# First mixer of a two-block transformer kernel: block-diagonal keys, one score product per unit

## Chip, cores and metric

One core of a Trainium2 chip runs the whole kernel. The time is the device time of one execution in microseconds; the lower it is the better. Three executions of the kernel before took 1032.47, 1033.88 and 1033.93 us, median 1033.88.

## What is computed

Two transformer blocks follow one another on 256 tokens of width 1024, all in float32. The change lies in the first block's mixer. Its one half is a differential attention of 4 heads. Each head has two sets of queries and keys of 64 dimensions, a rotary on the first 16 of them, and one set of values of 128:

```python
def block(qblk):                       # 128 queries at a time
    s = jnp.einsum('bqhmd,bkhmd->bhmqk', qblk, k)
    a = jax.nn.softmax(s, axis=-1)
    w = a[:, :, 0] - lam * a[:, :, 1]
    return jnp.einsum('bhqk,bkhe->bqhe', w, v)
```

There is no mask: every query sees all 256 keys. The mixer's other half is a gated linear recurrence (HGRN2, both directions), computed here in nine levels of blocks. Both halves are normalised per head, joined and multiplied by an output matrix. Then comes a gated feed-forward layer, a per-layer embedding gate and the second block.

## The kernel before

**Engines and queues.** The order of work is written out by hand, one program for each engine, with semaphores between them. Large matrices come through a ring of three slots (`raw`, 256 columns of a weight, 1 MB). ScalarE casts a slot to its high part (`hi`, line 497), VectorE subtracts to get the low part (`lo`, line 961), and TensorE multiplies high and low parts in fp32r with the high and low parts of the activations, three products for each tile. The next transfer into a slot starts when its low part is made. GpSimd casts one slot at the start (line 483) and is idle after that.

**Before the scores.** The input projection has 16 slots. The columns of `dq` and `dk` (slots 8 to 11) go transposed into `qT` and `kT`: 128 partitions hold the two 64-dimension sets of a head, with 4 heads and 256 tokens along the free dimension. TensorE puts one level of the recurrence behind each of the slots 6 to 13 (`level`, line 1915: eight float32 products of 128x128 by 128 columns) and the last two levels, 7 and 8, between the products of slot 14. VectorE prepares a level (`diffs`, `scaled`), and places the products into `AT` under a mask (`place`, line 1126). Log keys of the recurrence lie in `nb` under the name `kin`; the differences of level 7 (semaphore `lev_diff` at 8) read them last.

**Rotary.** `rotate(n)` on VectorE turns a pair of heads of `qT` (n = 0, 2) or `kT` (n = 1, 3) in place: a shuffle into `rot1`, two multiplications and an add (lines 1152 to 1155), all of 128 partitions by 512 elements. Rotations 0 and 1 stand in front of the placing of level 6, which TensorE's level 8 waits for; 2 and 3 stand behind the placings of levels 7 and 8, each in front of the maximum of unit 0 or 1.

**Units.** A unit n is a head (n // 2) and a block of 128 queries (n % 2); there are 8. Its two softmaxes share one PSUM bank, 256 columns each; two banks alternate. `scores(n, m)` (line 1927) multiplies the 64 partitions of set m. The second set's product waits for the first one's semaphore. VectorE takes the maxima of both sets in one reduction (`da_max`, line 1215); ScalarE takes two exponentials with sums (`da_exp`, line 668); VectorE makes two diagonal matrices of 1/sum and -lambda/sum (`da_diag`, lines 1219 to 1223); TensorE transposes and combines both sets by four float32 products with them (`da_pt`, line 1994); ScalarE copies the result (`da_copy`, line 677); TensorE multiplies by the values once both units of a head are there (`da_pv`, line 2002). A unit's score waits for the exponentials two units before.

**TensorE's order around it** (`scores` in two halves, at lines 2017 to 2048): behind slot 14 comes half (0,0), level 8, half (0,1); the gemm of slot 15 has two halves with score halves behind each; then the recurrence's outputs (`hg_out`, line 1977, 8 products of 256 columns); from there on score halves stand before and after the `da_pt` of two units earlier. Between them stand the recurrence's head means (`head_means`, line 1984: two products of 512 columns, each waiting for a square on ScalarE), `da_pv`, and from unit 4 on pieces of the output projection (`out_piece`, lines 1763 to 1765, 12 products each) that the recurrence alone feeds. In the end the attention's head means stand, and behind its norm the rest of the output projection.

Of the kernel before, what the change touches and what calls it, by code (L numbers as in the profile page):

```python
# [16 lines left out]
ALU = mybir.AluOpType  # L17
# [7 lines left out]
P = 128  # L25
# [108 lines left out]
def two_blocks(nc, A, out):  # L134
    with ExitStack() as ctx:
# [119 lines left out]
        lf = take(8, S)  # L255
        kin = nb
        E = take(8, TT, 129)
        qk = [take(2, 1024) for _ in range(2)]
# [8 lines left out]
        rot1 = adacc[:, :]  # L267
# [212 lines left out]
        @block.gpsimd  # L480
        def _(pool):
            pool.wait_ge(sem(f"raw{HI_POOL % 3}"), raw_count(HI_POOL))
            nc.gpsimd.tensor_copy(whi[HI_POOL % 3][:, :], raw[HI_POOL % 3][:, :]).then_inc(sem("hi_pool"), 1)

        @block.scalar
# [457 lines left out]
        def _(dve):  # L943
# [201 lines left out]

            def rotary(x, table, width, tmp):

                c = trig[:, table, 0, :]
                s = trig[:, table, 1, :]
                if width == 2:  # L1150
                    c, s = (v.unsqueeze(1).broadcast_to([P, 2, S]) for v in (c, s))
                link(v_.stream_shuffle(tmp, x, SWAP_I if table == 2 else SWAP_A))
                link(v_.tensor_tensor(tmp, tmp, s, ALU.mult))
                link(v_.tensor_tensor(x, x, c, ALU.mult))
                return v_.tensor_tensor(x, x, tmp, ALU.add)

            def rotate(n):

                x = (qT, kT)[n % 2][:, 2 * (n // 2):2 * (n // 2) + 2, :]
                dve.wait_ge(sem("in1_read_act"), (9, 11, 10, 12)[n])  # L1160
                if n:
                    dve.wait_ge(sem("rot1_done"), n)
                rotary(x, 0, 2, rot1.rearrange("p (a s) -> p a s", a=2)).then_inc(sem("rot1_done"), 1)

# [578 lines left out]
        def _(pe):  # L1743
# [174 lines left out]

            def scores(n, m):
                h, qt = n // 2, n % 2  # L1920
                pe.wait_ge(sem("rot1_done"), 4 if h > 1 else 2)
                if m == 0 and n >= 2:
                    pe.wait_ge(sem("da_exp"), 2 * (n - 2) + 2)
                if m == 1:
                    pe.wait_ge(sem("da_sc0"), n + 1)
                r = slice(64 * m, 64 * m + 64)
                pe.matmul(psX[:, 2 + n % 2, 256 * m:256 * m + 256], qT[r, h, P * qt:P * qt + P], kT[r, h, :],
                          start=(m == 0), stop=True, skip_group_check=True).then_inc(sem("da_sc" if m else "da_sc0"), 1)

# [87 lines left out]
            gemm_tok512(IN1 + 14, psX[:, 1, :], 0, 1).then_inc(sem("wt_used"), 1)  # L2017
            scores(0, 0)
            level(8)
            scores(0, 1)  # L2020
            gemm_tok512(IN1 + 15, psX[:, 0, :], 1, 0)
            scores(1, 0)
            gemm_tok512(IN1 + 15, psX[:, 1, :], 1, 1).then_inc(sem("wt_used"), 1)
            scores(1, 1)
            pe.wait_ge(sem("lev_placed"), nlev)
            hg_out(0)
            hg_out(1)
            scores(2, 0)
            da_pt(0)
            scores(2, 1)  # L2030
            pe.wait_ge(sem("in1_read_act"), 16)
            head_means("hg", lambda half: psX[:, half, :])
            scores(3, 0)
            da_pt(1)
            scores(3, 1)
            scores(4, 0)
            da_pt(2)
            scores(4, 1)
            da_pv(0)
            for n in range(3, 8):  # L2040
                if n < 6:
                    scores(n + 2, 0)
                da_pt(n)
                if n < 6:
                    scores(n + 2, 1)
                if n == 4:
# [386 lines left out]
```

## Time and profile before

| | |
|---|---|
| median of three executions | 1033.88 us |
| span of the profiled execution | 1032.9 us (its own time isn't given beside it) |
| TensorE busy, matmuls | 1004.6 us, 97% |
| VectorE busy | 792.5 us, 77% |
| ScalarE busy | 497.6 us, 48% |
| GpSimd busy | 3.0 us, 5 instructions |
| DMA | 199.93 MB, 194 GB/s in the mean |
| mean granted clock of TensorE | 0.993 |
| span of the changed part | about 120 to 170 us |

The busy times are read against the span, 1032.9 us. Matmuls overlap, so a busy matmul row isn't the engine's throughput: from the start of one to the start of the next is what it occupies. A row of a timeline gives the start in us from the span's start, the duration of the run of instructions in us, engine, line, operation, what is written and what is read, partitions by elements, and how many instructions were merged (xN). In brackets stand the idle time ahead and what ended it. `scr` is the big scratch region that holds `qT`, `kT`, `AT`, diagonals and exponentials. A float32 product is two MATMUL rows, an fp32r product one.

### The profile page before, as it was taken

How to read it: one execution, taken by the hardware profiler on the slowest of the kernel's cores; microseconds unless marked ns; L12 is line 12 of the kernel's file. 1: busy time of each engine (PE TensorE's matmuls, PEld its weight loads, DVE VectorE, ACT ScalarE, POOL GpSimd, SP SyncE). 2: the span in 40 equal slices, each digit the busy share in tenths (PEclk: the TensorE clock that was granted, in tenths of full speed). 3: DMA queues.
4: the chain of work that ended last, by engine and by line, in shares of the span. 5: the costliest groups of instructions: out<-in, count | busy, mean ns of one | idle time of the engine just before them, and what ended most of it. 6: DMA issues, size and time to landing. Idle time of an engine off the chain costs nothing.

```text
span 1032.9 us, 18856 instructions
## 1 busy us (share of the span) xinstructions
PE 1004.6 (97%) x7587; PEld 951.3 (92%) x7587; DVE 792.5 (77%) x1192; ACT 497.6 (48%) x595; POOL 3.0 (0%) x5
## 2 busy tenths in 40 slices
PE   6989999999999999999999999999999999999998
PEld 6989868899999999999999998988989999999997
DVE  6797972799989888799888887878954858654545
ACT  4787263543333445543434346555455464343341
POOL 1000000000000000000000000000000000000000
PEclk9999999999999999999999999999999999999999
DMA  7754321477786857399898956553332557755541
GB/s 239 229 170 124 121 82 43 164 239 246 246 263 224 266 182 246 121 303 343 291 322 289 320 177 158 169 163 115 93 121 89 171 169 229 251 194 176 190 162 41
DMA packets 163166, 199.93 MB, mean 194 GB/s; under 512 B 13232, under 2 KB 138154, under 8 KB 163114
## 3 DMA queue, kind: packets, MB, share of 16 engines
q1 hardware_dynamic: 163114, 199.20, 59.3%
q8 instruction: 38, 0.62, 0.3%
q14 instruction: 14, 0.11, 0.0%
HBM read 198.13 MB, written 1.05 MB: 193 GB/s over the span
## 4 chain that ended last, share of the span: by engine, by line
PE 73%; DVE 15%; issue 4%; ACT 4%; SPq 2%; DMA 1%; DVEq 0%; ACTq 0%
PE psX L1753 11%; PE psX L1758 11%; PE psX L1754 11%; PE psA L1758 4%; PE psA L1754 4%; PE psA L1753 4%; DVE wlo L961 3%; PE psX L1763 2%; PE psX L1764 2%; PE psX L1765 2%; PE psX L1810 2%; PE psA L1770 2%; PE psA L1771 2%; ACT whi L497 2%; PE psA L1772 2%
## 5 line engine op out<-in xcount | busy, mean ns | idle before, releaser
L961 DVE TENSOR_TENSOR wlo<-raw,whi 128x2048 fp32r<-128x2048 f32 x151 | 345.2, 2288 | 113.3 <-ACT whi L497 112.4
L497 ACT CAST whi<-raw 128x2048 fp32r<-128x2048 f32 x150 | 285.5, 1906 | 284.0 <-PE psX L1758 161.3
L1753 PE MATMUL psX<-hh,whi 128*128 128x256 f32 x1200 | 292.7, 284 | 0.8 <-ACT scr L598 0.8
L1754 PE MATMUL psX<-hl,whi 128*128 128x256 f32 x1200 | 291.1, 283 | 0.0
L1753 PEld LDWEIGHTS psX<-hh,whi 128*128 128x128 f32 x1200 | 230.3, 192 | 2.3 <-ACT scr L598 1.0
L1754 PEld LDWEIGHTS psX<-hl,whi 128*128 128x128 f32 x1200 | 230.3, 192 | 0.6 <-issue 0.2
L1758 PE MATMUL psX<-hh,wlo 128*128 128x256 f32 x1200 | 156.2, 283 | 0.0
L1758 PEld LDWEIGHTS psX<-hh,wlo 128*128 128x128 f32 x1200 | 149.4, 192 | 0.0
L1322 DVE SCALAR_TENSOR_TENSOR adacc<-scr,small,adacc 128x256 f32<-128x256 f32 (+1 forms) x175 | 105.4, 602 | 5.8
L1753 PE MATMUL psA<-oh,whi 128*128 128x256 f32 x320 | 77.7, 283 | 0.0
L1754 PE MATMUL psA<-ol,whi 128*128 128x256 f32 x320 | 77.7, 283 | 0.0
L1753 PEld LDWEIGHTS psA<-oh,whi 128*128 128x128 f32 x320 | 61.4, 192 | 0.0
L1754 PEld LDWEIGHTS psA<-ol,whi 128*128 128x128 f32 x320 | 61.4, 192 | 0.0
L1763 PE MATMUL psX<-hh,whi 128*128 128x256 f32 x200 | 60.3, 302 | 0.0
L1764 PE MATMUL psX<-hl,whi 128*128 128x256 f32 x200 | 56.5, 282 | 0.0
L1765 PE MATMUL psX<-hh,wlo 128*128 128x256 f32 x200 | 56.5, 282 | 0.0
L1800 PE MATMUL psX<-hh,whi 128*128 128x256 f32 x160 | 40.7, 293 | 5.1 <-ACT hh L524 3.4
L1758 PE MATMUL psA<-oh,wlo 128*128 128x256 f32 x320 | 41.7, 283 | 0.0
L1763 PEld LDWEIGHTS psX<-hh,whi 128*128 128x128 f32 x200 | 38.2, 191 | 3.4 <-issue 2.4
L1801 PE MATMUL psX<-hh,wlo 128*128 128x256 f32 x160 | 40.0, 289 | 0.0
L1758 PEld LDWEIGHTS psA<-oh,wlo 128*128 128x128 f32 x320 | 39.8, 192 | 0.0
L1764 PEld LDWEIGHTS psX<-hl,whi 128*128 128x128 f32 x200 | 38.2, 191 | 1.2 <-issue 1.2
(368 smaller groups left out, 1613.4 us busy)
## 6 DMA issues: line engine op xcount, KB each, us to landing
raw<-in_ffn_w SPq DMA_DIRECT2D x66, 1024.0 KB, 5.3
scr<-in_ada_w SPq DMA_DIRECT2D x36, 1024.0 KB, 7.4
raw<-in_w_in SPq DMA_DIRECT2D x33, 1024.0 KB, 5.5
raw<-in_w_ffn_gate SPq DMA_DIRECT2D x11, 1024.0 KB, 5.3
raw<-in_w_ffn_up SPq DMA_DIRECT2D x11, 1024.0 KB, 5.7
raw<-in_w_ffn_down SPq DMA_DIRECT2D x11, 1024.0 KB, 5.0
raw<-in_w_out SPq DMA_DIRECT2D x8, 1024.0 KB, 5.1
raw<-in_w_ple_gate SPq DMA_DIRECT2D x4, 1024.0 KB, 5.2
```

Of the source, the lines that this page charges most:

```text
L497: a_.copy(whi[b % 3][:, :], raw[b % 3][:, :]).then_inc(sem("hi_ready"), 1)
L961: v_.tensor_tensor(wlo[b % 3][:, :], raw[b % 3][:, :], whi[b % 3][:, :].bitcast(F32), ALU.subtract).then_inc(sem("lo_ready"), 1)
L1322: ins = v_.scalar_tensor_tensor(acc, w[:, k, :], c, acc, ALU.mult, ALU.add)
L1753: pe.matmul(dst, wh, xh, start=start, stop=False, skip_group_check=True)
L1754: pe.matmul(dst, wh, xl, start=False, stop=False, skip_group_check=True)
L1758: return pe.matmul(dst, w(kview(wlo[b % 3], kk)), xh, start=False, stop=stop, skip_group_check=True)
L1763: pe.matmul(dst, wh, xh, start=start, stop=False, skip_group_check=True)
L1764: pe.matmul(dst, wh, xl, start=False, stop=False, skip_group_check=True)
L1765: return pe.matmul(dst, wl, xh, start=False, stop=stop, skip_group_check=True)
L1770: pe.matmul(dst, xh, wh, start=start, stop=False, skip_group_check=True)
L1800: pe.matmul(dst, wh[:, k, P * t:P * t + P], hh[:, k, :], start=(k == 0 and t == 0), stop=False, skip_group_check=True)
L1801: pe.matmul(dst, wl[:, k, P * t:P * t + P], hh[:, k, :], start=False, stop=False, skip_group_check=True)
```

## The change

The keys of the attention are laid out block-diagonally. `kblk` takes the place of the recurrence's log keys in `nb`: for each head 2 x 256 columns, where the first 256 hold set 0 in partitions 0 to 63 and zeros below, and the last 256 hold zeros above and set 1 in partitions 64 to 127. GpSimd writes the zeros after the differences of level 7. VectorE's last add of rotations 1 and 3 goes in two instructions of 64 partitions into `kblk` instead of one of 128 into `kT`. A unit's score is one float32 product of all 128 partitions of `qT` with 512 columns of `kblk`. It takes the places of first halves in TensorE's order, except that score 0 stands behind level 8 and score 1 behind the first gemm half of slot 15; both halves' old semaphore between them goes.

```diff
--- before.py
+++ after.py
@@ -254,6 +254,7 @@
         hqT, gT = take(4, S), take(4, S)
         lf = take(8, S)
         kin = nb
+        kblk = nb[:, :, :].rearrange("p (h m) s -> p h m s", m=2)
         E = take(8, TT, 129)
         qk = [take(2, 1024) for _ in range(2)]
         AT = lf.rearrange("p (t h) s -> p t h s", t=TT)
@@ -481,6 +482,9 @@
         def _(pool):
             pool.wait_ge(sem(f"raw{HI_POOL % 3}"), raw_count(HI_POOL))
             nc.gpsimd.tensor_copy(whi[HI_POOL % 3][:, :], raw[HI_POOL % 3][:, :]).then_inc(sem("hi_pool"), 1)
+            pool.wait_ge(sem("lev_diff"), len(LEVELS) + 1)
+            for m in range(2):
+                nc.gpsimd.memset(kblk[64 * (1 - m):64 * (1 - m) + 64, :, m, :], 0.0).then_inc(sem("kblk_zero"), 1)
 
         @block.scalar
         def _(act):
@@ -1143,7 +1147,7 @@
                     place(n - 1)
 
 
-            def rotary(x, table, width, tmp):
+            def rotary(x, table, width, tmp, place=True):
 
                 c = trig[:, table, 0, :]
                 s = trig[:, table, 1, :]
@@ -1152,7 +1156,8 @@
                 link(v_.stream_shuffle(tmp, x, SWAP_I if table == 2 else SWAP_A))
                 link(v_.tensor_tensor(tmp, tmp, s, ALU.mult))
                 link(v_.tensor_tensor(x, x, c, ALU.mult))
-                return v_.tensor_tensor(x, x, tmp, ALU.add)
+                if place:
+                    return v_.tensor_tensor(x, x, tmp, ALU.add)
 
             def rotate(n):
 
@@ -1160,7 +1165,16 @@
                 dve.wait_ge(sem("in1_read_act"), (9, 11, 10, 12)[n])
                 if n:
                     dve.wait_ge(sem("rot1_done"), n)
-                rotary(x, 0, 2, rot1.rearrange("p (a s) -> p a s", a=2)).then_inc(sem("rot1_done"), 1)
+                tmp = rot1.rearrange("p (a s) -> p a s", a=2)
+                if n % 2 == 0:
+                    rotary(x, 0, 2, tmp).then_inc(sem("rot1_done"), 1)
+                    return
+                rotary(x, 0, 2, tmp, False)
+                dve.wait_ge(sem("lev_diff"), len(LEVELS) + 1)
+                for m in range(2):
+                    r = slice(64 * m, 64 * m + 64)
+                    ins = v_.tensor_tensor(kblk[r, 2 * (n // 2):2 * (n // 2) + 2, m, :], x[r], tmp[r], ALU.add)
+                ins.then_inc(sem("rot1_done"), 1)
 
             for j, (what, c0) in enumerate(IN1_COLS[:BESIDE1]):
                 if j not in (0, 5):
@@ -1916,16 +1930,14 @@
                                         start=True, stop=True, skip_group_check=True)
                 ins.then_inc(sem("lev_mm"), 1)
 
-            def scores(n, m):
+            def scores(n):
                 h, qt = n // 2, n % 2
                 pe.wait_ge(sem("rot1_done"), 4 if h > 1 else 2)
-                if m == 0 and n >= 2:
+                pe.wait_ge(sem("kblk_zero"), 2)
+                if n >= 2:
                     pe.wait_ge(sem("da_exp"), 2 * (n - 2) + 2)
-                if m == 1:
-                    pe.wait_ge(sem("da_sc0"), n + 1)
-                r = slice(64 * m, 64 * m + 64)
-                pe.matmul(psX[:, 2 + n % 2, 256 * m:256 * m + 256], qT[r, h, P * qt:P * qt + P], kT[r, h, :],
-                          start=(m == 0), stop=True, skip_group_check=True).then_inc(sem("da_sc" if m else "da_sc0"), 1)
+                pe.matmul(psX[:, 2 + n % 2, :].rearrange("p (m k) -> p m k", m=2), qT[:, h, P * qt:P * qt + P], kblk[:, h, :, :],
+                          start=True, stop=True).then_inc(sem("da_sc"), 1)
 
             def free(j):
 
@@ -2015,34 +2027,27 @@
             gemm_tok512(IN1 + 14, psX[:, 0, :], 0, 0)
             level(7)
             gemm_tok512(IN1 + 14, psX[:, 1, :], 0, 1).then_inc(sem("wt_used"), 1)
-            scores(0, 0)
             level(8)
-            scores(0, 1)
+            scores(0)
             gemm_tok512(IN1 + 15, psX[:, 0, :], 1, 0)
-            scores(1, 0)
+            scores(1)
             gemm_tok512(IN1 + 15, psX[:, 1, :], 1, 1).then_inc(sem("wt_used"), 1)
-            scores(1, 1)
             pe.wait_ge(sem("lev_placed"), nlev)
             hg_out(0)
             hg_out(1)
-            scores(2, 0)
+            scores(2)
             da_pt(0)
-            scores(2, 1)
             pe.wait_ge(sem("in1_read_act"), 16)
             head_means("hg", lambda half: psX[:, half, :])
-            scores(3, 0)
+            scores(3)
             da_pt(1)
-            scores(3, 1)
-            scores(4, 0)
+            scores(4)
             da_pt(2)
-            scores(4, 1)
             da_pv(0)
             for n in range(3, 8):
                 if n < 6:
-                    scores(n + 2, 0)
+                    scores(n + 2)
                 da_pt(n)
-                if n < 6:
-                    scores(n + 2, 1)
                 if n == 4:
                     da_pv(1)
                 if n == 6:
```

## Rows read from the trace of the kernel before

**Rows 1.** The page's part 4: the chain that ended last, share by engine.

```profile
PE 73%; DVE 15%; issue 4%; ACT 4%; SPq 2%; DMA 1%; DVEq 0%; ACTq 0%
```

**Rows 2.** Timeline of TensorE, 112 to 170 us.

```profile
112.94 1.95 PE L1915 MATMUL psA<-scr 128*128 128x128 f32 x16
114.65 0.48 PE L1770 MATMUL psX<-whi,hh 128*128 128x512 f32 x1
...
122.73 0.70 PE L1927 MATMUL psX<-scr 64*128 64x256 f32 x2 [0.56 <-DVE scr L1155]
123.97 2.05 PE L1915 MATMUL psA<-scr,ksum 128*128 128x128 f32 x16 [0.54 <-DVE scr L1126]
...
126.57 0.50 PE L1770 MATMUL psX<-whi,hh 128*128 128x512 f32 x1
...
133.77 3.72 PE L1977 MATMUL psA<-scr 128*128 128x256 f32 x16
137.42 0.70 PE L1927 MATMUL psX<-scr 64*128 64x256 f32 x2
138.05 1.16 PE L1994 MATMUL psA<-scr 128*128 128x128 f32 x8
139.14 0.70 PE L1927 MATMUL psX<-scr 64*128 64x256 f32 x2
139.76 1.98 PE L1984 MATMUL psX<-scr,ones 128*128 128x512 f32 x4
141.68 0.70 PE L1927 MATMUL psX<-scr 64*128 64x256 f32 x2
...
143.39 0.70 PE L1927 MATMUL psX<-scr 64*128 64x256 f32 x4
...
151.25 0.75 PE L1927 MATMUL psX<-scr 64*128 64x256 f32 x2 [1.16 <-ACT scr L668]
151.94 2.07 PE L1994 MATMUL psA<-scr 128*128 128x128 f32 x8
...
169.50 1.98 PE L1984 MATMUL psA<-scr,ones 128*128 128x512 f32 x4
```

**Rows 3.** By stretch (granted clock third from the end); TensorE's timeline elsewhere.

```profile
151.50:152.00 0.50, 0.50 (x3) 0.07 (x2) 0.50 (x3) 0.50 (x1) 0.00 (x0) 0.71 0.00 0
...
158.50:159.00 0.50, 0.50 (x6) 0.50 (x5) 0.00 (x0) 0.00 (x0) 0.00 (x0) 0.97 1.09 389
...
66.30 3.68 PE L1915 MATMUL psA<-scr 128*128 128x128 f32 x16 [3.12 <-DVE scr L1116]
...
175.59 0.39 PE L1763 MATMUL psX<-oh,whi 128*128 128x256 f32 x1 [1.25 <-DVE ol L1241]
...
625.41 0.36 PE L1800 MATMUL psX<-hh,whi 128*128 128x256 f32 x1 [2.17 <-ACT hh L524]
```

**Rows 4.** Timeline of VectorE, 110 to 145 us.

```profile
110.38 0.70 DVE L1110 TENSOR_TENSOR scr<-nb,scr 128x512 f32<-128x512 f32 x1
...
121.98 0.69 DVE L1155 TENSOR_TENSOR scr<-scr,adacc 128x512 f32<-128x512 f32 x1
122.59 2.77 DVE L1126 COPY_PREDICATED scr<-con,psA 128x512 f32<-128x512 int32 x4
...
133.88 0.69 DVE L1215 TENSOR_REDUCE scr<-psX 128x2 f32<-128x512 f32 x1 [0.39 <-PE psX L1927]
...
144.12 0.69 DVE L1215 TENSOR_REDUCE scr<-psX 128x2 f32<-128x512 f32 x1 [0.71 <-PE psX L1927]
```

**Rows 5.** Timeline of ScalarE, 134 to 140 us.

```profile
134.60 0.47 ACT L668 ACTIVATE scr<-psX,scr 128x256 f32<-128x256 f32 x1 [2.98 <-DVE scr L1215]
...
138.26 1.11 ACT L643 ACTIVATE scr<-psA 128x512 f32<-128x512 f32 x2
```

**Rows 6.** Timelines of GpSimd and VectorE, 12 to 16 us.

```profile
13.27 2.82 POOL L483 CAST whi<-raw 128x2048 fp32r<-128x2048 f32 x1 [12.82 <-DMA raw<-in_w_in]
...
12.05 2.29 DVE L961 TENSOR_TENSOR wlo<-raw,whi 128x2048 fp32r<-128x2048 f32 x1 [0.59 <-ACT whi L497]
```

## Prediction

> **What bounds the kernel now.** I read the chain of waits first: TensorE carries nearly three quarters of it, VectorE much of the rest [rows 1]. So a saving counts only where TensorE itself is last, and the change touches 50 of 1033 us. I therefore read the timelines of that stretch, one engine at a time.
>
> On TensorE a half score (64 rows, 256 columns) standing alone takes 0.63 us from its start to the next (137.42 to 138.05) [rows 2]. The same traffic in 128 rows shows what a column costs: the level block of eight 128-column products fills 112.94 to 114.65, so 1.71 us or 1.67 ns a column; 256 columns are 0.43 us and 0.20 us of the 0.63 is something else. The block behind a half score pays too: four 128-column products should take 0.86 us and take 1.09 (138.05 to 139.14), and two 512-column ones 1.92 instead of 1.71 (139.76 to 141.68). A visit of the 64-row form costs about 0.4 us beyond its columns. There are 15 such visits for 16 halves, for at 143.39 two halves of different units stand together, and their four instructions take the 0.70 us that the two of a lone half do.
>
> TensorE waits in three places there: 0.56 us for the key rotary and 0.54 us for a placed level (122.73, 123.97), and 1.16 us before the first half of unit 6, for ScalarE's exponentials (151.25) [rows 2, 3]. After the last of these the granted clock falls to half between 151.5 and 152.0 us and is back between 158.5 and 159.0 [rows 3]; the same eight products of unit 4 take 2.0 us instead of 1.09 [rows 2]. The half-speed stretch is 6.8 us long and costs 3.4.
>
> VectorE has no idle time from 115 to 133.5 us: rotary, placing, maxima [rows 4]. ScalarE between 134.6 and 139.4 does exp, two copies, a cast, two squares in one string, and TensorE's mean products wait for those squares [rows 5].
>
> **The change, part by part.**
>
> *Keys' last add split in two* (unit pairs 1 and 3 of the rotary). VectorE's time goes by elements per partition, and each new add has the 512 of the old one on half the partitions. The old takes 0.69 us, and the next instruction starts 0.61 behind it (121.98 to 122.59) [rows 4]. So +0.60 us twice; bounds 0.3 (if partitions counted) and 0.69. Queued behind the first is placing of level 6, whose end frees level 8 on TensorE: 123.97 becomes 124.57. Behind the second is the maximum of unit 1, which idled 0.39 us before: 133.88 becomes 134.6, and ScalarE's string with it (squares done at 140.1 instead of 139.4).
>
> *The new wait of VectorE on the level differences* costs nothing: these end at 111.1 us [rows 4]. *GpSimd's two zero fills* start then, 1024 elements a partition each. The one GpSimd row casts 2048 in 2.82 us [rows 6]; by elements the fills take 2.8 us together, bounds 1 and 5.6, and end by 117. TensorE needs them at 126.3: 9 us of cover. If the cover went, each us past 126.3 would be a us for TensorE, with the last gemm of the projections queued behind.
>
> *The score as one product.* 512 columns at 1.67 ns are 0.86 us; bounds 0.85 and 1.26 (two halves as they are now). I take 0.87, as nothing around it is in 64 rows any more. For the same reason the neighbours fall by 0.2 each: 0.86 for a transposing block, 1.71 for the means, 3.43 for the mixer outputs (3.65 now); bounds 0 and 0.24. The Trainium skill, TensorEngine Tiling (Array Packing), Key Properties, has a rule against this change: row tiles operate independently, so two halves in the two row groups run side by side. The trace agrees at 143.39, 0.70 us of busy time for two as for one; by that rule that one visit loses 0.23 us with the change, which is in the sum.
>
> *The order.* Score 0 now stands behind level 8. TensorE ends its gemm at 122.17 (122.73 less 0.56) and idles to 124.57: 2.4 us in one piece where there were 0.56 and 0.54 with a product between. Does the clock hold? An idle time of 3.12 us was followed by half speed (the same level block 3.68 us for 1.95), one of 2.17 us too [rows 3]; each time one stretch of 3.4 us, which costs 1.7. I expect a fall here.
>
> **The sum.** Without a fall: level 8 from 124.57 (1.79 with the step to the gemm), score 0 0.87, gemm at 127.2 (126.57 now); its two halves 5.52 (7.20 from 126.57 to 133.77 less two visits of 0.84) and score 1 0.87, done at 133.6; outputs done at 137.05 against 137.42. With the fall +1.6: 138.65. Then score 2 and block 0, 1.73, and the means, 1.71: 142.1 against 141.68 (141.4 without a fall, for then the squares are last). So by 142 us nothing is gained: +0.4.
>
> From there score 3 is 0.87 and whole at 143.0, where its second half now came behind block 1 and held VectorE's maximum of unit 3 until 144.12, after 0.71 idle [rows 4]. That maximum moves to 143.1, 1.0 earlier, and with it all behind it on VectorE: four scaling operations, the diagonals of unit 3, two subtractions, the maximum of unit 4, then ScalarE's exp. Score 6 waits for that exp: 151.25 becomes 150.2. TensorE is through block 3 at 148.2 and idles 2.0 us. **First term: -1.05 us** (-1.8 without the first fall).
>
> From score 6 to the attention means TensorE takes 18.25 us now (151.25 to 169.50). Off come the 3.4 of the clock and 1.5 for units 6 and 7 (four visits of 0.84, the first 0.1 cheaper behind idle time, less two products of 0.87); on come about 1.0 of waits that the slow clock hid (the value product of head 1 waits for a copy behind ScalarE's weight cast, 0.3, and short ones for diagonals). That is 14.35 us: -3.9. Then I expect the 2.0 us idle to bring one stretch of 3.4 us at half speed, as the 2.17 us one did, not two as now: +1.7. **Second term: -2.2 us.** Behind the means the tail of ScalarE and VectorE and all later weights follow in the same order, fed by transfers that start when a ring slot is free, so the gain is kept. Sum -3.25. The sum is made against the span of 1032.9; the execution's own time isn't given, and the median of the runs is 1.0 above that span. I carry that distance: 1033.88 - 3.25 = 1030.6.
>
> **The rivals.**
>
> *A. The clock holds at the second wait, or at both.* For it: 1.25 us of idle time at 175.59 cost nothing, and the work around the wait no longer has 64-row products in it [rows 3]. Against: 2.17 us did. It gives -4.95 (1028.9), or -5.7 (1028.2) if both hold.
>
> *B. The second low stretch is 6.8 us as now.* TensorE was busy through the first half of that stretch and stayed slow, with 64-row and 128-column products; of these only the first kind goes. Then +1.7: -1.55, 1032.3, which is no change that shows. The same comes out if the neighbours keep their 0.2 and score and diagonal chains on VectorE are last anyway.
>
> *C. Slower: the zero fills are late.* Score 0 waits for both, and everything on TensorE stands behind it. By rows they have 9 us of cover. The mechanism: GpSimd gets no access while VectorE works without a break, which is until VectorE itself runs out of scores, after the third rotary at 128.7. Two fills at the cast's full 2.82 then end at 134.3, 8.0 after need: +8.0 - 3.25, about 1038.6. The case is slower by over 0.2% from an end of the fills at 131.6 on (126.3 + 3.25 + 2.07). Against: the cast of 2.82 us ran while VectorE subtracted, at 2.29 us, its usual 2.288 [rows 6]. The Trainium skill, GPSIMD Engine Reference, says that GpSimd shares its SBUF interfaces with VectorE and contends with VectorE instructions that have two SBUF inputs; rotary and scaling have two. By that rule the fills stretch. The trace shows no stretch of VectorE's, and can't show that of GpSimd's.
>
> *D. The saving is real and TensorE isn't last.* The product form gives its 5.7 us of TensorE time (15 visits of 0.84 against 8 products of 0.87), but ScalarE's string and VectorE's extra adds set each meeting point, and the rest is lost as idle time. That is partly in my sum already, in the first term; in full it gives -1 to 0 us.
>
> **How the numbers follow.** A measurement of this kernel can tell 0.2%, 2.1 us. My case 0.42 (1030.6), A 0.30, B 0.12, D 0.09, C 0.05, and 0.02 for both falls being long, about +0.2 to +3. My case and A are faster by over 0.2%, all but 0.01 at the edge: 0.71. B, D, that 0.01 and half of the last 0.02: 0.23. C and the other half: 0.06. The range reaches from A with a term to spare (1027.5) through B and D up to 1034.0; C is left out.
>
> **What would show it.** Right: no 64-row score on TensorE; eight scores of some 0.87 us, blocks behind them at 0.86; TensorE idle 2.4 us before level 8; maximum of unit 3 near 143; the attention means near 166 instead of 169.5. The granted clock after 124 and after 150 us tells my case from A and B. Wrong: a score of 1.2 us or neighbours still at 1.09 (the 0.2 isn't of the 64-row form); a wait of score 0 on GpSimd (C); an end of the stretch at 168.5 or later with TensorE idle for ScalarE (D); a gain above 7 us, which would mean that I missed a wait that the halves made.

## The result, and the profile after

The changed kernel took 1029.29 us in the median of 7 runs (1027.48 to 1031.22), beside 1033.93 for 7 runs of the kernel before. The medians lie 4.6 us apart. The estimated ratio, which the comparisons here go by, is smaller: 0.9965, 95% interval 0.9951 to 0.9979, so 3.6 us less (2.2 to 5.1). The forecast was 1030.6. A second set of 8 runs (the first experiment) gave 0.9975 (0.9965 to 0.9986), 2.6 us less.

The profiled execution has a span of 1025.7 us against 1032.9, a time of 1027.48. It is the fastest of its seven, so its span overstates the gain; the two profiles also differ by a stretch of 3.4 us at half clock near 626 us, far behind the change, that only the one of before has. The chain of the page's part 4 has barely moved:

```profile
PE 72%; DVE 15%; ACT 5%; issue 4%; DMA 2%; SPq 1%; DVEq 0%; ACTq 0%
```

TensorE's timeline around the change. The one product is line 1939; 1929 is the level block, 1989 the recurrence's outputs, 2006 the transposing block, 1996 head means:

```profile
123.23 3.26 PE L1929 MATMUL psA<-scr,ksum 128*128 128x128 f32 x16 [2.60 <-DVE scr L1130]
126.29 1.51 PE L1939 MATMUL psX<-nb,scr 128*128 128x512 f32 x2
...
130.40 1.02 PE L1939 MATMUL psX<-nb,scr 128*128 128x512 f32 x2
...
134.02 3.62 PE L1989 MATMUL psA<-scr 128*128 128x256 f32 x16
137.47 1.02 PE L1939 MATMUL psX<-nb,scr 128*128 128x512 f32 x2
138.33 1.05 PE L2006 MATMUL psA<-scr 128*128 128x128 f32 x8
139.22 1.88 PE L1996 MATMUL psX<-scr,ones 128*128 128x512 f32 x4
140.94 1.02 PE L1939 MATMUL psX<-nb,scr 128*128 128x512 f32 x2
...
149.12 1.10 PE L1939 MATMUL psX<-nb,scr 128*128 128x512 f32 x2 [1.79 <-ACT scr L672]
...
163.18 1.98 PE L1996 MATMUL psA<-scr,ones 128*128 128x512 f32 x4
```

A score is 0.86 us from its start to the next (137.47 to 138.33), a transposing block 0.89 (1.09 in [rows 2]), the two head means 1.72 (1.92). No 64-row product is left. TensorE waits twice: 2.60 us before level 8 and 1.79 before score 6. Level 8 took 3.06 us (123.23 to 126.29), most of it at half clock, which lasts from about 123.9 to 127.3. The second wait brought no fall. The stretches show both; the granted clock is third from the end:

```profile
123.50:124.00 0.50, 0.50 (x6) 0.50 (x6) 0.50 (x2) 0.00 (x0) 0.00 (x0) 0.85 0.00 0
124.00:124.50 0.50, 0.50 (x4) 0.50 (x4) 0.50 (x2) 0.00 (x0) 0.00 (x0) 0.50 0.00 0
127.00:127.50 0.50, 0.50 (x3) 0.25 (x1) 0.43 (x1) 0.00 (x0) 0.00 (x0) 0.74 0.00 0
...
149.00:154.00 5.00, 4.88 (x28) 3.83 (x28) 4.48 (x9) 3.50 (x8) 0.00 (x0) 1.00 0.00 0
```

VectorE (1156 is a rotary's shuffle, 1176 the two adds, 1130 the placing, 1229 a maximum) and GpSimd:

```profile
115.15 0.76 DVE L1156 STREAM_SHUFFLE adacc<-scr 128x512 f32<-128x512 f32 x1
...
120.44 1.39 DVE L1176 TENSOR_TENSOR nb<-scr,adacc 64x512 f32<-64x512 f32 x2
121.85 2.77 DVE L1130 COPY_PREDICATED scr<-con,psA 128x512 f32<-128x512 int32 x4
...
127.83 0.69 DVE L1229 TENSOR_REDUCE scr<-psX 128x2 f32<-128x512 f32 x1 [0.40 <-PE psX L1939]
...
133.99 0.69 DVE L1229 TENSOR_REDUCE scr<-psX 128x2 f32<-128x512 f32 x1
...
142.00 0.69 DVE L1229 TENSOR_REDUCE scr<-psX 128x2 f32<-128x512 f32 x1
```

```profile
109.60 1.96 POOL L487 MEMSET nb<- 64x1024 f32 x2 [93.48 <-DVE scr L1114]
```

Level 8, which the placing of level 6 frees (the first half of the row at 121.85), and the maxima of units 0, 1 and 3 (127.83, 133.99, 142.00) follow the adds. The two adds stand 1.41 us ahead of the next instruction, where the one add stood 0.61 [rows 4]. The zero fills end at 111.6, 15 us before score 0. Times from the start of the span can't be compared between profiles as they stand, since stretches of half clock near 66 us, 3.4 us long in some profiles and 6.8 in others, shift what is behind them. So I take VectorE's first rotary shuffle as the origin from here on and call the time from there to TensorE's attention means **the way**: 52.81 us before (116.69 to 169.50), 48.03 after (115.15 to 163.18).

### The profile page after: what moved, and what is told of

Read it like the earlier page. It is cut to its first block, busy times and chain, and to the rows that moved or that the text cites. A ratio compares the mean times of both kernels' runs of the same rounds, so it can differ in the third digit from the quotient of the medians.

```text
span 1025.7 us, 18824 instructions
## 1 busy us (share of the span) xinstructions
PE 995.9 (97%) x7571; PEld 945.9 (92%) x7571; DVE 793.9 (77%) x1194; ACT 498.5 (49%) x595; POOL 5.0 (0%) x7
## 3 DMA queue, kind: packets, MB, share of 16 engines
HBM read 198.13 MB, written 1.05 MB: 194 GB/s over the span
## 4 chain that ended last, share of the span: by engine, by line
PE 72%; DVE 15%; ACT 5%; issue 4%; DMA 2%; SPq 1%; DVEq 0%; ACTq 0%
PE psX L1767 11%; PE psX L1772 11%; PE psX L1768 11%; PE psA L1772 4%; PE psA L1768 4%; PE psA L1767 4%; DVE wlo L965 3%; PE psX L1777 2%; PE psX L1778 2%; PE psX L1779 2%; ACT whi L501 2%; DMA raw<-in_w_in 2%; PE psX L1824 2%; PE psA L1784 2%; PE psA L1785 2%
```

## The experiments

A low stretch is one at half clock (granted clock 0.5). "Level 8", "max 3" and "score 6" are starts of these from the origin.

| kernel | level 8 | head means | max 3 | score 6 | way | low in the way | ratio of times (95%) |
|---|---|---|---|---|---|---|---|
| before | 7.28 | 23.07 | 27.43 | 34.56 | 52.81 | 6.8 us | 1 |
| after | 8.08 | 24.07 | 26.85 | 33.97 | 48.03 | 3.4 | 0.9965 (0.9951-0.9979) |
| again | 8.06 | 24.05 | 26.83 | 33.95 | 48.01 | 3.4 | 0.9975 (0.9965-0.9986) |
| before_warm | 7.25 | 23.00 | 27.36 | 34.48 | 49.67 | none | 0.9982 (0.9970-0.9994) |
| order_only | 7.28 | 23.97 | 27.33 | 34.45 | 49.48 | none | 0.9981 (0.9967-0.9996) |
| rows128 | 8.07 | 23.49 | 27.24 | 34.36 | 49.14 | none | 0.9974 (0.9958-0.9991) |
| pairs | 7.26 | 21.87 | 25.38 | 32.50 | 50.04 | 3.4 | 0.9981 (0.9965-0.9997) |
| score0_first | 8.06 | 23.47 | 26.33 | 33.44 | 47.50 | none | 0.9966 (0.9951-0.9981) |
| warm | 8.08 | 23.51 | 26.36 | 33.49 | 47.55 | none | 0.9963 (0.9948-0.9977) |
| fill | 8.07 | 23.49 | 26.34 | 33.46 | 47.52 | none | 0.9966 (0.9953-0.9979) |
| one_add | 7.24 | 21.84 | 24.69 | 31.80 | 45.86 | none | 0.9947 (0.9931-0.9962) |
| pool_add | 8.41 | 25.62 | 28.47 | 35.59 | 49.66 | 6.8 | 0.9976 (0.9963-0.9989) |
| reorder | 4.07 | 20.26 | 25.28 | 32.39 | 46.46 | none | 0.9963 (0.9950-0.9976) |
| max_early | 4.09 | 20.27 | 25.29 | 31.21 | 45.27 | none | 0.9953 (0.9937-0.9970) |

In the last two a placing of 1.23 us stands ahead of the origin instead of behind it; add 1.2 to every one of their starts and to their ways to compare them. There is one profile of each kernel, two of the changed one.

**again**: no edit.

> The changed kernel unaltered, as the base of this set. I follow one stretch in every run: from the start of TensorE's level 6 (eight products) to the start of the attention means. It was 56.56 us before and 51.78 in the first profile of the change. The form theory (the 64-row form costs 0.4 us a visit beyond its columns, the product of 128 rows none) expects products of 0.86 us, blocks behind them of 0.89, and a stretch of 51 to 54 us, by how often the clock falls to half: each fall of 3.4 us costs up to 1.7. The luck theory (most of the gain was the fall after the second wait that didn't come in that profile) expects 53.5 or more in this run and a time within 2 us of the kernel before.

The stretch from level 6 was 51.79 us (112.36 to 164.15), the way 48.01: the same to 0.02 as in the first profile, in a run 2.3 us longer. What differed lies outside: a low stretch near 620 us that the first profile lacked. The median is 1030.97 us against 1033.55, and the stretch 51.79 where the luck theory wanted 53.5 or more: it fails.

**order_only**: the kernel before, with both halves where the change has its product.

```diff
             scores(2, 0)
+            scores(2, 1)
             da_pt(0)
-            scores(2, 1)
...
```

> The old keys, rotary and two products of 64 rows, but in the changed order: both halves of a unit stand together, in one bank, the second waiting for the first. Form theory: a visit takes 1.1 to 1.3 us and the block behind it keeps its 0.2 us; the unit 3 maximum comes 0 to 0.5 us earlier in the stretch than before, not 1.0 to 1.7; stretch 55 to 56.5 us with a fall of the clock at the second wait, 52.5 to 53.5 without. Order theory (what gained was that a unit's score is whole before the block of the unit two before): the stretch is within 0.5 us of the changed kernel's at equal falls, and the time equals that of the changed kernel.

TensorE's timeline of this run:

```profile
142.35 1.51 PE L1927 MATMUL psX<-scr 64*128 64x256 f32 x4
143.79 1.16 PE L1994 MATMUL psA<-scr 128*128 128x128 f32 x8
```

A visit takes 1.44 us (142.35 to 143.79), more than I gave it: the second half waits for the first one's end. The maximum of unit 3 moves 0.1 us against before. Without a low stretch its way is 49.48, the old order's is 49.67 (before_warm, below). So the order alone gains 0.2 us of way. That its time is 0.9981 of before's goes with the clock: TensorE's wait before score 6 is down to 0.14 us (151.02, behind a block that ends at 150.88), no low stretch follows it, and the mean granted clock of its ten runs is 0.9965, of the 21 of before beside them 0.9943. The order theory fails as to the way.

**before_warm**: to see what the clock cost before, five dummy products in the old kernel's 1.16 us wait.

```diff
             for n in range(3, 8):
+                if n == 4:
+                    for _w in range(5):
+                        pe.matmul(psX[:, 0, :], zeros[:, :], zeros[:, 0:1].broadcast_to([P, 512]), ...)
                 if n < 6:
                     scores(n + 2, 0)
```

> The kernel before with five dummy bf16 products of 512 columns in the wait in front of the first half of score 6, where 1.16 us of idle time was followed by 6.8 us at half clock. If that idle time brings the clock down, it holds, and the way from VectorE's first rotary to the attention means falls from 52.8 us to 49.4 to 50.0; the changed kernel needs 48.0 with a fall near 124 us and 47.5 without one. Then 1.9 to 2.5 us of the change's gain is its own and what is more comes from the clock; the time lies 0 to 2 us under the kernel before. If the many short 64-row products bring the clock down by themselves, the fall comes again and the way stays at 52 us or more.

```profile
149.12 1.26 PE L2043 MATMUL psX<-zeros 128*128 128x512 bf16 x5
150.35 0.67 PE L1927 MATMUL psX<-scr 64*128 64x256 f32 x2
151.03 1.16 PE L1994 MATMUL psA<-scr 128*128 128x128 f32 x8
```

Score 6 comes 0.1 us earlier than before and the block behind it takes 1.09 us (151.03 to 152.12) instead of 2.0; the way is 49.67 and the time 1031.09, 0.9982 (0.9970 to 0.9994). One profile without a fall could be chance, but the mean granted clock of the twelve runs is 0.9966, of the 29 of before beside them 0.9942. The fall cost 3.1 us of way in the profile, and the runs are 1.9 us shorter in the mean. So of the 4.78 us between the two profiles' ways 3.1 is the old kernel's fall, 0.5 goes back for the new one at level 8 (warm, below), and 2.1 to 2.2 (49.67 to 47.5) is the change's own. The times say the same within their intervals: score0_first and warm (below), changed kernels without the new fall, have 0.9966 and 0.9963, before_warm 0.9982, some 1.7 to 2.0 us apart.

**rows128**: the old order and sixteen halves, each as 128 rows by 256 columns of the block-diagonal keys.

```diff
-                r = slice(64 * m, 64 * m + 64)
-                pe.matmul(..., qT[r, h, P * qt:P * qt + P], kT[r, h, :], ...)
+                pe.matmul(..., qT[:, h, P * qt:P * qt + P], kblk[:, h, m, :], ...)
```

> The old order with sixteen halves, but each half is a product of all 128 rows with the 256 columns of its set in the block-diagonal keys (so with the changed rotary and zero fills). Form theory, now: what saves TensorE time is that no 64-row product stands between 128-row ones. A half takes 0.43 to 0.46 us, the block behind it 0.86 to 0.89, and the stretch from level 6 to the attention means is 51 to 52 us without a fall of the clock, like the changed kernel's 51.8 (one fall), against 53.2 with both 64-row halves together. Fusing theory (one wait and one instruction pair less, or a whole score ahead of the block, is what saves): the stretch is 53 us or more without a fall.

```profile
136.49 0.59 PE L1941 MATMUL psX<-nb,scr 128*128 128x256 f32 x2
136.92 1.05 PE L2008 MATMUL psA<-scr 128*128 128x128 f32 x8
137.81 0.60 PE L1941 MATMUL psX<-nb,scr 128*128 128x256 f32 x2
139.76 1.96 PE L1998 MATMUL psX<-scr,ones 128*128 128x512 f32 x4 [1.35 <-ACT scr L647]
```

A half takes 0.43 us (136.49 to 136.92) where the 64-row one took 0.63, the block behind it 0.89 where it took 1.09. The overhead is the form's, 0.2 us going in and 0.2 coming out. By the Trainium skill, TensorEngine Tiling (Array Packing), Key Properties, a change of tiling mode drains TensorE. The 0.2 us on each side agree with that; no run tells a drain from another cost of the form. TensorE then waits 1.35 us for ScalarE's squares. And the way is 49.14, not 47.5: the stretch from level 6 is 52.04, at the edge between what the theories gave. In the old order the maximum of unit 3 is 0.9 us later than with whole scores (27.24 against 26.35), and what VectorE and ScalarE do behind it goes with it. The split adds cost 1.6 us in the changed order (one_add, below); that they cost as much here wasn't measured at the end of the way, but the maximum of unit 1 is as late here as in warm (18.34 and 18.36 from the origin, 17.12 in before_warm). Taken so, the parts are: 64 rows to 128 in the old order -2.1, whole scores and their order a further -1.6 (order_only, in 64 rows, gave -0.2), adds +1.6. The two theories each had a part of it.

**pairs**: the old 64-row halves, ordered so that the second half of a unit stands directly ahead of the first of the next, in another bank.

```diff
             scores(3, 1)
             scores(4, 0)
             da_pt(2)
             scores(4, 1)
+            scores(5, 0)
             da_pv(0)
...
```

> The old keys and 64-row halves, without zero fills or split adds, in an order in which the second half of a unit always stands directly in front of the first half of the next unit, in another bank: nine visits for sixteen halves. If two halves in different row groups run side by side wherever they meet, a visit of two takes 0.63 us and VectorE's string is 1.2 us shorter than in the changed kernel, so that the stretch is 50.5 to 52 us without a fall of the clock. If the meeting at 143.39 in the old profile was a chance, a visit takes 1.1 us or more and the stretch is above 52.5.

```profile
140.13 0.70 PE L1927 MATMUL psX<-scr 64*128 64x256 f32 x4
140.76 1.16 PE L1994 MATMUL psA<-scr 128*128 128x128 f32 x8
...
147.98 0.67 PE L1927 MATMUL psX<-scr 64*128 64x256 f32 x2 [1.17 <-ACT scr L668]
...
155.83 1.16 PE L1994 MATMUL psA<-scr 128*128 128x128 f32 x8 [1.43 <-DVE scr L1223]
```

Two halves in different row groups take 0.63 us together (140.13 to 140.76, four instructions) wherever they meet back to back: the row of 143.39 was no chance. Up to score 6 this kernel is ahead of the change (32.50 against 33.5). Then it loses: the clock falls to half behind a wait of 1.17 us, and unit 5's block waits 1.43 us for VectorE's diagonals, which in VectorE's order stand behind the maximum of unit 6, and that waits 2.48 us for the late half score of TensorE. Its way is 50.04 and its time 0.9981. The part on concurrency came out. The part on the way didn't: the stretch from level 6 is 53.8 us, so at least 52.1 without the fall, against 50.5 to 52; whether a better order of the tail would beat the change wasn't tried.

**score0_first** and **warm**: the first puts score 0 in front of level 8, the second eleven dummy products.

```diff
+            scores(0)
             level(8)
-            scores(0)
```

> The changed kernel with score 0 in front of level 8, as the first half was before. If the piece of 2.6 us idle is what brings the clock down near 124 us, the wait is split in about 1.3 and 0.4 to 0.5 us with a product between, the clock holds there, level 8 takes 1.7 to 2.0 us instead of 3.06, and the recurrence outputs start 1.5 to 2 us earlier, but the attention means only 0 to 0.7 us earlier, because the head means then wait for ScalarE's squares. If the fall has another cause, it comes here too and the stretch stays.

> The changed kernel with eleven dummy bf16 products of 512 columns (some 2.4 us) in the wait in front of level 8. They compute nothing that is used. If the piece of 2.6 us idle brings the clock down, it holds now near 125 us, level 8 takes 1.7 to 2.0 us and the recurrence outputs start 1.6 us earlier; but the means wait for ScalarE's squares, so that the attention means come only 0.4 to 0.6 us earlier (51.3 in the stretch, as with score 0 in front). If the fall cost more than its place on TensorE shows, the stretch is 51 or less.

```profile
121.56 2.57 PE L2031 MATMUL psX<-zeros 128*128 128x512 bf16 x11
124.34 2.05 PE L1929 MATMUL psA<-scr,ksum 128*128 128x128 f32 x16 [0.21 <-DVE scr L1130]
126.22 1.02 PE L1939 MATMUL psX<-nb,scr 128*128 128x512 f32 x2
...
139.77 1.96 PE L1996 MATMUL psX<-scr,ones 128*128 128x512 f32 x4 [0.93 <-ACT scr L647]
```

In both the clock holds, as was expected if the wait brings it down. In warm level 8 takes 1.88 us (124.34 to 126.22). The recurrence's outputs start 1.7 us (warm) and 2.5 us (score0_first, where 2 at most was expected) earlier, and most of it is waiting time again at the head means, 0.93 and 1.76 us, for ScalarE's squares. The way shortens by 0.5 us. In warm's seven runs the mean granted clock was 0.9969, in the fifteen of the changed kernel 0.9940, so the new wait seems to cost clock in most runs; only the profiles show where.

**fill**: an output piece moved into the wait before score 6.

```diff
+                if n == 4:
+                    pe.wait_ge(sem("hg_olo"), 2)
+                    out_piece(0, 0, range(4, KT), True, False)
                 if n < 6:
                     scores(n + 2)
...
-                if n == 4:
-                    pe.wait_ge(sem("hg_olo"), 2)
-                if 4 <= n < 8:
+                if 5 <= n < 8:
```

> The changed kernel with the first piece of the output projection, 12 products, moved in front of score 6, into the 1.79 us that TensorE waits there for ScalarE. If the piece's own inputs (ready at 147.3 in the changed profile) come in time, TensorE's wait shrinks to some 0.3 us on either side of it, score 6 is 0 to 0.2 us later, and all behind comes 1.3 to 1.6 us earlier: stretch 50.2 to 50.6 with one fall of the clock. Also there is no idle time left that could bring the clock down at this place. Rival: the diagonals and exponentials of units 5 to 7 become the bound and the stretch shrinks by less than 0.5 us.

```profile
148.03 0.39 PE L1777 MATMUL psX<-oh,whi 128*128 128x256 f32 x1
...
149.78 1.10 PE L1939 MATMUL psX<-nb,scr 128*128 128x512 f32 x2
...
152.76 1.10 PE L1939 MATMUL psX<-nb,scr 128*128 128x512 f32 x2
155.05 1.16 PE L2006 MATMUL psA<-scr 128*128 128x128 f32 x8 [1.19 <-DVE scr L1237]
```

The piece fits, score 6 isn't late (33.46), score 7 comes 1.4 us earlier than in warm (152.76, and 154.12 there, origins 0.06 apart). Then unit 5's block waits 1.19 us for VectorE's diagonals and the way is 47.52: nothing gained. The rival was right. VectorE is last there with a weight subtraction of 2.3 us between maxima 5 and 6.

**one_add**: of the two adds in each key rotation only that of set 0 is made, so the keys of set 1 are not computed.

```diff
-                for m in range(2):
+                for m in range(1):
                     r = slice(64 * m, 64 * m + 64)
                     ins = v_.tensor_tensor(kblk[r, ...], x[r], tmp[r], ALU.add)
```

> The changed kernel with the second of the two 64-partition adds left out in both key rotations, so set 1 of the keys is wrong. If the extra add is on the path (my step: 0.60 us in front of level 8 and 1.2 us in front of the unit 1 maximum), level 8 starts 0.6 us earlier behind the gemm (idle 2.0 instead of 2.6 us) and the attention means start 0.4 to 0.7 us earlier in the stretch at equal falls of the clock. If VectorE's extra work is hidden, the stretch stays within 0.2 us of the changed kernel's.

```profile
120.65 0.68 DVE L1176 TENSOR_TENSOR nb<-scr,adacc 64x512 f32<-64x512 f32 x1
121.26 2.75 DVE L1130 COPY_PREDICATED scr<-con,psA 128x512 f32<-128x512 int32 x4
```

A lone add of 64 partitions stands 0.61 us ahead of the placing (120.65 to 121.26), as the old one of 128 did; the pair stands 1.41. Level 8 starts 0.8 us earlier and the way is 45.86, 1.6 us under the 47.5 of the changed kernels without a low stretch. A second add costs 0.8, and both reach the end in full: more than the 0.4 to 0.7 us expected.

**pool_add**: set 1's add on GpSimd.

```diff
+            for i in range(2):
+                pool.wait_ge(sem("rot_mul"), i + 1)
...
+                nc.gpsimd.tensor_tensor(kblk[64:128, 2 * i:2 * i + 2, 1, :], x, tmp, ALU.add).then_inc(sem("pool_add"), 1)
...
-                for m in range(2):
+                for m in range(1):
```

> The changed kernel with the add of set 1 in both key rotations on GpSimd, beside VectorE's add of set 0 and what follows. With both left-out adds the way from the first rotary to the attention means was 45.9 us against 47.5 in runs of the changed kernel without a fall of the clock. If GpSimd's add takes some 1 to 1.5 us (64 partitions, 512 elements, two inputs) it is done before the scores need it, VectorE isn't slowed, and the way is 46 to 46.5 us (plus 0.5 with a fall near 124 us): the time some 1.5 us under the changed kernel's. If GpSimd and VectorE hinder one another when both read two tensors, the placing or rotary beside it takes longer (0.69 becomes 0.9 or more) and the way stays at 47 us or more.

GpSimd's add, and VectorE beside it:

```profile
121.19 1.26 POOL L492 TENSOR_TENSOR nb<-scr,adacc 64x512 f32<-64x512 f32 x1 [8.92 <-DVE scr L1164]
```

```profile
120.42 0.69 DVE L1164 TENSOR_TENSOR scr<-scr,trig 128x512 f32<-128x512 f32 x1
121.22 1.79 DVE L1187 TENSOR_TENSOR nb<-scr,adacc 64x512 f32<-64x512 f32 x1
122.93 2.74 DVE L1135 COPY_PREDICATED scr<-con,psA 128x512 f32<-128x512 int32 x4
```

GpSimd's add takes 1.26 us, and VectorE's own add of 64 partitions beside it 1.79 instead of the 0.68 of one_add: it ends 0.6 us behind GpSimd's. The second pair does the same, 1.29 and 1.81 us. What stretched is this add, not the placing behind it. So VectorE loses 1.71 us (121.22 to 122.93) where the two adds took 1.41, the unit 1 maximum is 1.6 us later than in the change, the wait before level 8 grows to 2.95 us with 6.8 us of half clock behind it. The way stays above 47, as expected of the two hindering one another. The Trainium skill, GPSIMD Engine Reference, section 1 (Specifications), says that GpSimd contends with VectorE instructions with two SBUF inputs; these rows agree.

**reorder**: the placing of level 6 in front of the rotations, ScalarE's squares in front of its cast.

```diff
-            hi(IN1 + 17)
             norm_square(("hg", "hg_o"), 0, 1)
             norm_square(("hg", "hg_o"), 1, 2)
+            hi(IN1 + 17)
...
+                if n >= 3:
+                    place(n - 1)
                 if n == nlev - 2:
                     rotate(0)
                     rotate(1)
-                if n >= 3:
-                    place(n - 1)
```

> The changed kernel with the placing of level 6 in front of the rotations 0 and 1 on VectorE, and ScalarE's squares of the recurrence in front of its second weight cast. If the 2.6 us of TensorE's wait before level 8 is only a matter of VectorE's order, level 8 follows the gemm directly and score 0 waits 0.5 to 1.5 us for the rotary: no fall of the clock near 124 us, recurrence outputs at 15.5 to 16.5 us from the first rotary or earlier, head means at 21.5 to 22.5 instead of 24.1. What is behind is partly bound by VectorE, which does the same work: attention means 0.5 to 2 us earlier. If VectorE's and ScalarE's strings alone set the end, the way stays within 0.3 us of 47.5.

```profile
120.89 1.95 PE L1929 MATMUL psA<-scr,ksum 128*128 128x128 f32 x16
123.53 1.13 PE L1939 MATMUL psX<-nb,scr 128*128 128x512 f32 x2 [0.69 <-DVE nb L1176]
```

Level 8 follows the gemm without a wait. Head means come 2.6 us earlier by a common origin (20.26 + 1.23 against 24.07), and the attention means not at all: 47.69 by that origin against 47.5. VectorE's string sets the end: the maximum of unit 3 stands at 26.5 by that origin, in warm at 26.4. The clock is the highest of all versions, 0.9972 in the mean of twelve runs and none under 0.995. The time, 1028.95 us and 0.9963 (0.9950 to 0.9976), can't be told from the changed kernel's.

**max_early**: reorder, with the maximum of unit 4 ahead of two subtractions.

```diff
+            da_max(4)
             for half in range(2):
                 norm_lo("hg", half, 4)
-            da_max(4)
```

> The reorder kernel with the maximum of unit 4 in front of the two subtractions of the recurrence's output on VectorE (1.2 us together). In all runs of the changed form TensorE waits 1.79 us before score 6 for ScalarE's exponentials of unit 4, and these for that maximum, whose score is done 3 us earlier. If VectorE's order is the bound there, the wait shrinks to 0.5 to 0.7 us, all behind comes 1.1 to 1.3 us earlier (45.2 to 45.4 us from the first rotary to the attention means, against 46.46), and there is neither wait left that brought the clock down: median 1 to 1.5 us under the reorder kernel's, so some 0.9950 of the kernel before. If ScalarE's own string (two casts, a copy, then exp) is last there, the wait shrinks by less than 0.5 us.

```profile
148.54 1.10 PE L1939 MATMUL psX<-nb,scr 128*128 128x512 f32 x2 [0.59 <-ACT scr L672]
```

The wait before score 6 falls from 1.79 to 0.59 us and the way by 1.19, to 45.27, as VectorE's order being the bound would have it. The median is 0.7 us under reorder's, less than the 1 to 1.5 expected: 1028.24, 0.9953 (0.9937 to 0.9970): the fastest version here that computes the whole reference, though its interval overlaps the changed kernel's.

## Why the prediction was right, point by point

*Form and price of the product*: right. Score 0.86 (I took 0.87), blocks behind it 0.89 (0.86), outputs 3.45 (3.43), means 1.72 (1.71). rows128 shows that it is the form that costs.

*The split adds*: mis-sized. I took 0.60 each from the distance of one such add to the next instruction; it is 0.80 at level 8 and 1.65 in the unit 1 maximum (18.84 from the origin against 17.19; I had 0.72). The pair stands 1.41 us ahead of the next instruction, each for its full duration of about 0.70, without the 0.08 overlap. The Trainium skill, VectorE: DVE Perf Modes, section on two Vector instructions with no wait between them, has an instruction held until the earlier ones are done when its operands start in another group of 32 partitions; set 1 starts at partition 64. The rows agree (one_add has the 0.61 us back when only the set at partition 0 is added), and no run tells this cause from another. So 1.65 is twice 0.80, less the 0.39 us that unit 1's maximum used to idle, and 0.40 more for unit 0's, which waited for score 0 behind the slow level 8 (127.83); in warm, without the fall, unit 1's maximum is 0.48 us earlier. That wait I hadn't in the sum.

*Fills hidden, rival C*: the cover held, 15 us of it. They took 1.96 us together, less than my 2.8, while VectorE ran an elementwise product of two SBUF inputs that took the 1.24 us it took before (at 109.43, and at 110.98 before). So these fills and VectorE didn't hinder one another. The contention that C rests on exists for other work: pool_add shows it between two adds.

*First fall*: right, in both profiles of the kernel, and worth 0.5 us at the end of the way (48.0 against 47.5), where my two sums differ by 0.75.

*First term, -1.05 to score 6*: -0.59. The direction and the link (maximum of unit 3 freed from a late half) were right; the adds took 0.4 us more than I gave them, and TensorE's wait was 1.79 us where I had 2.0.

*Second term, -2.2*: -4.19 in the profile (14.06 against 18.25), since the second fall didn't come. That is rival A: I had -3.9 for it and -4.95 in all. None of the seven profiles with a wait of 1.78 or 1.79 us there shows a fall behind it, while before and pairs fell behind 1.16 and 1.17 us; in those two 64-row products stand around the wait. The step that failed is that the wait of 2.0 us would bring the clock down as one of 2.17 us had. That one, near 620 us [rows 3], was a draw: it stands with 2.16 or 2.17 us in all fourteen profiles of this case, and the clock fell behind it in six (before, again, order_only, rows128, pool_add, max_early) and held in eight. Here it is in after, where the clock held, and in again, the same kernel, where it fell (0.50 from 619.9 to 623.4):

```profile
619.13 0.36 PE L1814 MATMUL psX<-hh,whi 128*128 128x256 f32 x1 [2.17 <-ACT hh L528]
620.06 0.55 PE L1814 MATMUL psX<-hh,whi 128*128 128x256 f32 x1 [2.16 <-ACT hh L528]
```

So a single row of a trace can't show that a wait brings the clock down, and what decides it stays open.

*The sum*: -3.25 forecast, -3.6 and -2.6 measured in two sets (-4.6 between the medians of the first, nearer to A's 1028.9). That the number came out is in part luck. The adds cost 0.4 us more than I gave them and the second fall didn't come; and the profile of before, from which I took the old fall, was one of the lower-clocked half: among 89 runs of the kernel before whose clock is known 46 had a mean clock of 0.9935 or less, among 15 of the changed kernel 8. At that clock the means are 1034.3 and 1031.2 us; between 0.9955 and 0.9975 they are 1031.9 (29 runs) and 1029.2 (5 runs). So the clock's share about cancels over many runs, and 2.6 to 3.1 us is left for the change, beside the 2.2 that the way without falls shows. The 0.4 to 0.9 us between them lie within the intervals of the runs.

*Rival D*: half true. With one add in place of two the way is 3.8 us under the old one (45.86 against 49.67), less than the 5.7 of TensorE time that the form saves; the second adds take 1.6 of it back, and fill and reorder show that what else TensorE saves in this stretch is lost to VectorE's order. *Rival B*: didn't come.

## What to carry to other kernels

Count what a product of another array form costs at its two neighbours, not only itself: here 0.4 us for each visit of a 64-row float32 product among 128-row ones, so that multiplying zeros was cheaper. When the saving is on one engine and the price on another, price the second by its pitch in the new form; and when a wait is moved, look at which engine's order makes it, since filling TensorE's wait with other work gained nothing of the way, while moving one maximum forward in VectorE's queue gained 1.2 us (reordering the placing and the rotations gained none). And a fall of the clock seen once behind a wait is no price: the same wait of 2.17 us had one in six of fourteen profiles.

## What the runs showed of the hardware that I had not expected

- A VectorE add of 64 partitions by 512 took 1.79 us instead of 0.68 while a GpSimd add of the same shape ran, which took 1.26.
- Two VectorE adds that start at partitions 0 and 64 follow one another at their full 0.70 us, where an add followed by an instruction that starts at partition 0 as well is over 0.61 us later, with 0.08 of overlap.
- Two 64-row halves in one bank, the second waiting for the first, take 1.44 us; in two banks and without a wait between, 0.63.
- The same wait doesn't always do the same to the clock: 2.17 us near 620 us was followed by half clock in six profiles of fourteen. Nor does its length order it: 1.16 us and 1.17 us ahead of score 6 were followed by half clock, seven waits of 1.78 or 1.79 us there and three of 1.71 to 1.79 us ahead of level 8 (fill, one_add, order_only) weren't; 2.60, 2.61 and 2.95 us ahead of level 8 were.
- A GpSimd fill of 64 partitions by 1024 float32 takes 1.0 us (two in 1.96), a cast of 128 by 2048 from 2.76 to 3.24 in fourteen profiles.
